# Layer 0 up-projection: normalized operand from its sixteenth unit on, evictions by ScalarE, eight modulation pieces moved to VectorE

## The reference, cut to what matters

```python
for i in range(DEPTH):                                   # DEPTH = 2
    mod = c_act @ w_mod[i] + b_mod[i]                    # six vectors of 1024
    sh1, sc1, g1, sh2, sc2, g2 = jnp.split(mod, 6, axis=-1)
    h = modulate(rmsnorm(x, norm_mix[i]), sh1, sc1)      # h * (1 + scale) + shift
    y = pool_mixer(...) if i % N_MIXERS == 0 else moba_attention(...)
    x = x + g1[:, None, :] * y
    h = modulate(rmsnorm(x, norm_mlp[i]), sh2, sc2)
    x = x + g2[:, None, :] * squared_relu_mlp(h, w_up[i], w_down[i])   # relu(h @ w_up)^2 @ w_down
```

## Time and profile before

| what | value |
|---|---|
| median of 3 runs | 1028.49 us (1027.91 to 1028.98) |
| the profiled execution, its own time | 1028.39 us |
| its span, first to last instruction | 1026.6 us, so 1.8 us lie around it |
| TensorE busy | 989.7 us, 96% of the span |
| VectorE busy | 780.7 us, 76% |
| ScalarE busy | 527.2 us, 51% |
| DMA moved | 222.28 MB, mean 217 GB/s |
| granted TensorE clock, mean | 0.989 of full |

### The profile page before, as it was taken

One profiled execution on the slowest core, in us unless ns is written; L12 is line 12 of the kernel. 1 busy time (PEld: TensorE's weight loads), 2 busy tenths in 40 slices (PEclk: granted clock), 3 DMA queues, 4 the chain that ended last, 5 costly groups with the idle time before them and its releaser, 6 DMA issues.

```text
span 1026.6 us, 19924 instructions
## 1 busy us (share of the span) xinstructions
PE 989.7 (96%) x7918; PEld 939.0 (91%) x7918; DVE 780.7 (76%) x1430; ACT 527.2 (51%) x834; POOL 1.9 (0%) x14
## 2 busy tenths in 40 slices
PE   4789999999999999999999999999999999999996
PEld 1469999999998899999999989898889999999996
DVE  4659666888767778778765889899987787777554
ACT  4247655444666566764544535468116565444343
POOL 0000000000000000000000000000000000000000
PEclk9799999999999999999999999999999999999998
DMA  9998977877464865544555436363445555555531
GB/s 376 421 421 298 365 301 275 329 305 277 136 210 126 302 245 170 197 169 164 206 203 193 137 124 244 103 228 124 164 152 200 183 173 202 200 175 193 205 124 42
DMA packets 35880, 222.28 MB, mean 217 GB/s; under 512 B 3883, under 2 KB 9180, under 8 KB 9436
## 3 DMA queue, kind: packets, MB, share of 16 engines
q1 hardware_dynamic: 35804, 221.22, 59.9%
HBM read 220.13 MB, written 1.07 MB: 215 GB/s over the span
## 4 chain that ended last, share of the span: by engine, by line
PE 93%; DMA 3%; DVE 2%; ACT 1%; issue 1%; SPq 0%; DVEq 0%; ACTq 0%
PE bank L591 24%; PE bank L597 24%; PE bank L592 24%; PE bank L923 11%; PE bank L972 3%; PE s_banks L620 2%; DMA mod_raw<-w_mod 1%; PE s_banks L972 1%; DMA raw<-weights 1%; PE s_banks L597 1%; PE s_banks L591 1%; PE s_banks L592 1%; DMA x<-x_in 0%; DVE s L1519 0%; PE bank L853 0%
## 5 line engine op out<-in xcount | busy, mean ns | idle before, releaser
L1403 DVE TENSOR_TENSOR w_lo<-raw,w_hi 128x1024 fp32r<-128x1024 f32 x268 | 324.6, 1217 | 32.0 <-ACT w_hi L1043 31.2
L1043 ACT ACTIVATE w_hi<-raw 128x1024 fp32r<-128x1024 f32 x268 | 280.1, 1051 | 110.6 <-PE bank L597 104.1
L591 PE MATMUL bank<-xg_hi,w_hi 128*128 128x258 f32 (+1 forms) x1248 | 310.4, 286 | 2.3 <-DVE w_lo L1403 2.3
L592 PE MATMUL bank<-xg_lo,w_hi 128*128 128x258 f32 (+1 forms) x1248 | 306.1, 282 | 0.0
L591 PEld LDWEIGHTS bank<-xg_hi,w_hi 128*128 128x128 f32 x1248 | 235.9, 189 | 6.8 <-issue 6.6
L592 PEld LDWEIGHTS bank<-xg_lo,w_hi 128*128 128x128 f32 x1248 | 236.4, 189 | 0.2
L597 PE MATMUL bank<-xg_hi,w_lo 128*128 128x258 f32 (+1 forms) x1248 | 180.8, 283 | 0.0
L597 PEld LDWEIGHTS bank<-xg_hi,w_lo 128*128 128x128 f32 x1248 | 162.8, 189 | 0.0
L591 PE MATMUL bank<-hid_hi,w_hi 128*128 128x256 f32 x512 | 123.5, 279 | 0.0
L592 PE MATMUL bank<-hid_lo,w_hi 128*128 128x256 f32 x512 | 123.4, 279 | 0.0
L1807 DVE SCALAR_TENSOR_TENSOR y<-u,vec,y 128x256 f32<-128x256 f32 x240 | 98.4, 477 | 0.2
(11 more groups left out here) (238 smaller groups left out, 1256.6 us busy)
## 6 DMA issues: line engine op xcount, KB each, us to landing
raw<-weights SPq DMA_DIRECT2D x157, 1024.0 KB, 5.0
mod_raw<-w_mod SPq DMA_DIRECT2D x32, 1024.0 KB, 11.4
mod_raw<-w_dots SPq DMA_DIRECT2D x16, 1024.0 KB, 8.1
toep<-bias_by_distance SPq DMA_DIRECT2D x8, 256.0 KB, 5.4
x<-x_in SPq DMA_DIRECT2D x1, 1024.0 KB, 4.9
toep<-bias_by_distance SPq DMA_DIRECT2D x8, 128.0 KB, 3.9
y_out<-yout SPq DMA_DIRECT2D x4, 256.0 KB, 2.5
c_all<-c_row SPq DMA_DIRECT2D x1, 512.0 KB, 7.6
```

Source lines behind the costliest of these rows:

```text
L591: pe.matmul(dst, hi, r_hi, start=start, stop=False, skip_group_check=True)
L592: pe.matmul(dst, hi, r_lo, start=False, stop=False, skip_group_check=True)
L1043: act.activation(pool_w_hi[:, at, :] if name == "pool" and at < 2 else w_hi[:, at % HL, :], raw[:, slot, (at % 2) * UT * P:(at % 2 + 1) * ...
L1403: ve.tensor_tensor(lo, raw[:, slot, (at % 2) * UT * P:(at % 2 + 1) * UT * P], hi.bitcast(F32), ALU.subtract).then_inc(lo_done, 1)
```

## The change

- Constants: `NORMED = 15`. From the sixteenth unit of `up0` (number 15) on, the operand is `xn_hi`, `xn_lo`, which hold the normalized, scaled and shifted x (256 columns). VectorE multiplies (`xn_product(k)`, end of step 6+k), ScalarE adds the shift and rounds (`xn_high(k)`, start of step 7+k), VectorE subtracts (`xn_low(k)`, start of step 7+k), for k = 0 to 7.
- For these 17 units VectorE's `evict` is gone; ScalarE's relu reads the PSUM bank, and a bank is free when the relu is done.
- In both `up` phases ScalarE makes `hid_hi` by a second square of `ub`, in place of VectorE's copy.
- Eight of the twelve row pieces of `up0` become dots in `up0`, after units 15, 17, 19, 20, 22, 24, 26, 29. The four that stay rows are done one at a time after units 16, 21, 25, 28. `c_all` is loaded after pair 5 and activated after unit 5.
- `xn_hi`, `xn_lo` lie where slots 3 and 4 of `mod_raw` were, so from piece 20 to piece 34 there are three slots; the order of the issues (PIECES_AFTER) is new.

```diff
+NORMED = 15
-MOD_AT = {("up0", 12): HEAD, ("up0", 20): HEAD + 1, ("up0", 28): HEAD + 2}
+ROW_AT = {("up0", 16): 0, ("up0", 21): 1, ("up0", 25): 2, ("up0", 28): 3}
+COPY_AT = {("up0", 28): HEAD}
+COLS_AT = {("up0", 30): HEAD}
+DOTS_AT = {("up0", v): d for d, v in enumerate((15, 17, 19, 20, 22, 24, 26, 29))}
+for kind in "drdddrddrdrd":                 # pieces 20 to 31: d = dots, r = row
+SLOT = [q % SLOTS for q in range(MOD_FIRST)] + [n % 3 for n in range(15)] + [(n + 3) % SLOTS for n in range(15, 28)]
-PIECES_AFTER = [5, 6, 7, 8, 10, 11, 12, 13, 14, 15, 16, 17, 18, 19, 20, 22, 23, ...
+PIECES_AFTER = [6, 7, 8, 14, 14, 15, 16, 16, 17, 17, 18, 19, 19, 20, 21, 22, 23, ...
...
@@ TensorE, bank_free, whole
+                elif name == "up0" and 8 * i + j >= NORMED + 4:
+                    pe.wait_ge(relu_done, 8 * i + j - 3)
                 for k in range(DC):
+                    if ready is not None:        # unit 15: xn_lo_done
+                        pe.wait_ge(ready, k + 1)
@@ ScalarE
+            def xn_high(k):
+                act.wait_ge(xn_mul, k + 1)
+                act.activation(xn_hi[:, k, :], newt[:, k % 2, :], ACT.Identity, bias=modv[...8 * SH2 + k...]).then_inc(xn_hi_done, 1)
             def up(name, i, j):
+                if name == "up0" and 7 <= 8 * i + j < 7 + DC:
+                    xn_high(8 * i + j - 7)
+                if name == "up0" and 8 * i + j >= NORMED:
+                    act.wait_ge(pe_units, U0[name] + 8 * i + j + 1)
+                    act.activation(ub[:, j % 2, :], out_bank(name, 8 * i + j)[:, 0:SEQ], ACT.Relu).then_inc(relu_done, 1)
+                else: (as before)
                 act.wait_ge(relu_done, 8 * i + (base + j + 1))
+                act.activation(chunk(hid_hi, 8 * i + j), ub[:, j % 2, :], ACT.Square).then_inc(hid_hi_done, 1)
+                if name == "up0" and 8 * i + j >= NORMED:
+                    act.wait_ge(hid_lo_done, 8 * i + j - 1)
                 act.activation(sb2[:, j % 2, :], ub[:, j % 2, :], ACT.Square).then_inc(sq2_done, 1)
@@ VectorE
             def hidden(name, i, j):
+                ve.wait_ge(hid_hi_done, 8 * i + (base + j + 1))
                 ve.wait_ge(sq2_done, 8 * i + (base + j + 1))
-                ve.tensor_copy(chunk(hid_hi, t), sb2[:, j % 2, :]).then_inc(hid_hi_done, 1)
+            def xn_product(k):
+                ve.scalar_tensor_tensor(newt[:, k % 2, :], x[:, k, :], gain[:, 1, k:k + 1], rstd[:, 0:SEQ], ALU.mult, ALU.mult).then_inc(xn_mul, 1)
+            def xn_low(k):
+                ve.wait_ge(xn_hi_done, k + 1)
+                ve.scalar_tensor_tensor(xn_lo[:, k, :], newt[:, k % 2, :], modv[...8 * SH2 + k...], xn_hi[:, k, :].bitcast(F32), ALU.add, ALU.subtract).then_inc(xn_lo_done, 1)
             def up(name, i, j):
-                evict(name, i, j)
                 t = 8 * i + j
+                if name == "up0" and 7 <= t < 7 + DC:
+                    xn_low(t - 7)
+                if name == "up1" or t < NORMED:
+                    evict(name, i, j)
                 (split as before)
                 hidden(name, i, j)
+                if name == "up0" and 6 <= t < 6 + DC:
+                    xn_product(t - 6)
```

More of the change, by code:

```diff
@@ L63, in _phases @@
         else:
-            by_vector += GLU_SPLIT if name == "glu" else t
+            by_vector += {"glu": GLU_SPLIT, "up0": NORMED}.get(name, t)
     return units
@@ L187, in rows_of @@
     return [(kinds, p) for p in range(ROWS)] if g is None else [(8 * kind, g) for kind in kinds]
[L190 to L195, removed]
+DOTS = [(48 + 8 * kind, p) for kind in (SC2, SH2) for p in range(4)]\
+    + [(base, p) for p in range(4) for base in (8 * G2, 48 + 8 * SC1, 48 + 8 * SH1)]\
+    + [(48 + 8 * G2, p) for p in range(4)]
+DOTS_AT = {("up0", v): d for d, v in enumerate((15, 17, 19, 20, 22, 24, 26, 29))}
+DOTS_AT.update({("down0", 8 * p + at): 8 + 3 * p + n for p in range(4) for n, at in enumerate((1, 2, 5))})
+DOTS_AT.update({("down1", 8 * p): 20 + p for p in range(4)})
+PIECES = [("rows", q) for q in range(MOD_FIRST)]
+for kind in "drdddrddrdrd":
+    PIECES.append(("dots", sum(k == "dots" for k, _ in PIECES)) if kind == "d" else ("rows", sum(k == "rows" for k, _ in PIECES)))
+PIECES += [("dots", d) for d in range(8, 24)]
+NORMED_SLOTS = (3, 4)
+SLOT = [q % SLOTS for q in range(MOD_FIRST)] + [n % 3 for n in range(15)] + [(n + 3) % SLOTS for n in range(15, 28)]
+BEFORE = [max([p for p in range(q) if SLOT[p] == SLOT[q]], default=None) for q in range(len(PIECES))]
+IN_SLOT = [sum(SLOT[p] == SLOT[q] for p in range(q + 1)) for q in range(len(PIECES))]
 ROWS_PIECE = [n for n, (kind, _) in enumerate(PIECES) if kind == "rows"]
 DOTS_PIECE = [n for n, (kind, _) in enumerate(PIECES) if kind == "dots"]
-PIECES_AFTER = [5, 6, 7, 8, 10, 11, 12, 13, 14, 15, 16, 17, 18, 19, 20, 22, 23, 24, 26, 27, 28, 30, 31, 32, 48, 49, 50, 51]
+PIECES_AFTER = [6, 7, 8, 14, 14, 15, 16, 16, 17, 17, 18, 19, 19, 20, 21, 22, 23, 24, 26, 27, 28, 30, 31, 32, 48, 49, 50, 51]
 def pieces_after(p):
@@ L252, in build @@
         cz = sb("cz", [P, DC, 64], F32, first)
-        mod_raw = sb("mod_raw", [P, SLOTS, DC * SEQ], F32, first)
+        mod_raw = sb("mod_raw", [P, 3, DC * SEQ], F32, first)
+        with ExitStack() as part:
+            mod_raw2 = sb("mod_raw2", [P, 2, DC * SEQ], F32, part)
+        half_line("xn", first)
+        xn_hi = sb("xn_hi", [P, DC, SEQ], F32R, first)
+        xn_lo = sb("xn_lo", [P, DC, SEQ], F32R, first)
+        piece_slot = [mod_raw[:, s, :] for s in range(3)] + [mod_raw2[:, s, :] for s in range(2)]
         c_all = sb("c_all", [P, D], F32, first)
@@ L360, in build @@
         relu_done = sem("relu_done")
+        xn_mul, xn_hi_done, xn_lo_done = sem("xn_mul"), sem("xn_hi_done"), sem("xn_lo_done")
         sq2_done = sem("sq2_done")
@@ L468, in piece @@
             def piece(q):
-                (kind, n), s = PIECES[q], q % SLOTS
-                if q >= SLOTS:
-                    before, m = PIECES[q - SLOTS]
+                (kind, n), s = PIECES[q], SLOT[q]
+                if BEFORE[q] is not None:
+                    before, m = PIECES[BEFORE[q]]
+                    if s in NORMED_SLOTS and BEFORE[q] < MOD_FIRST <= q:
+                        sp.wait_ge(pe_units, U0["down0"])
                     if before == "rows":
@@ L477, in piece @@
                 src = w_mod if kind == "rows" else w_dots
-                sp.dma_start(mod_raw[:, s, :], src[one(n)].rearrange("a p n -> p (a n)")).then_inc(mod_in[s], 16)
+                sp.dma_start(piece_slot[s], src[one(n)].rearrange("a p n -> p (a n)")).then_inc(mod_in[s], 16)
             def pair(p, s, base=0):
@@ L620, in row @@
                     mm = pe.matmul(row_bank[32 * c:32 * c + 32, 0:SEQ], cz[:, k, 31 - r:63 - r],
-                                   mod_raw[:, n % SLOTS, SEQ * k:SEQ * (k + 1)], start=r == 0 and k < 4,
+                                   piece_slot[SLOT[n]][:, SEQ * k:SEQ * (k + 1)], start=r == 0 and k < 4,
                                    stop=r == ROW_COUNT[b] - 1 and k >= 4, tile_position=(0, 32 * c), skip_group_check=True)
@@ L640, in mod_work @@
             def mod_work(name, v):
-                if (name, v) in MOD_AT:
-                    rows(MOD_AT[name, v])
+                if (name, v) in ROW_AT:
+                    row(HEAD, ROW_AT[name, v])
                 if (name, v) in COLS_AT:
@@ L773, in down @@
                 dst = out_bank(name, j // 4)
-                if j % 4 == 0:
+                if name == "down0" and i == 0 and j % 4 == 0:
+                    pe.wait_ge(relu_done, 29 if j == 0 else 32)
+                elif j % 4 == 0:
                     pe.wait_ge(tile_read, 2 * i + (T0[name] + j // 4 - (1 if not isinstance(i, int) or i or j else 3)))
@@ L804, in step @@
                 def step(i, j):
-                    whole(name, i, j, xg_hi, xg_lo, SEQ + 2)
+                    v = 8 * i + j
+                    if name == "up0" and v >= NORMED:
+                        whole(name, i, j, xn_hi, xn_lo, SEQ, xn_lo_done if v == NORMED else None)
+                    else:
+                        whole(name, i, j, xg_hi, xg_lo, SEQ + 2)
                     if isinstance(i, int):
-                        mod_work(name, 8 * i + j)
+                        mod_work(name, v)
                 unrolled = 32 if name == "up0" else 16
@@ L1053, in mod_work @@
             def mod_work(name, v):
-                if (name, v) in MOD_AT:
-                    mod_copy(MOD_AT[name, v])
-                if (name, v) == ("up0", 16):
+                if (name, v) in COPY_AT:
+                    mod_copy(COPY_AT[name, v])
+                if (name, v) == ("up0", 5):
                     act.wait_ge(c_row_in, 16)
```

22 lines of the change are left out of this document (12 added, 10 removed).

## The result

| | before | after |
|---|---|---|
| median (range, runs) on one chip | 1028.47 us (1027.91 to 1028.98, 5) | 1034.38 us (1032.69 to 1034.94, 5) |
| profiled execution, its own time | 1028.39 us | 1032.69 us |
| its span and mean granted clock | 1026.6 us, 0.989 | 1030.9 us, 0.983 |

The ratio is 1.0058 [1.0047, 1.0070]: slower, as forecast. The medians differ by 5.9 us, the profiled executions by 4.3; that of after is the fastest of its five. The forecast was 1037.3 in 1030 to 1042.

A forecast was written before the change was run, and what follows sets the result against it. TensorE was taken as the bound, 93% of the chain. Savings -9.4, loop stall +11.2, clock +1.7, late piece +3.6, clock +1.7 gave +8.8 us on 1028.39: forecast 1037.3 us, range 1030.0 to 1042.0.

The forecast's parts named there:

- The loop: up0 steps 7 to 14, VectorE and ScalarE waiting in turn: 3.58 us a turn, TensorE stalls 11.2 us up to unit 15.
- The late piece: up0 row 21 waits for piece 25, behind pair 15: stall 5.3 us, 3.6 after the first clock loss.
- Savings: TensorE in up0: fewer rows and columns, -8.3 us, and 17 units at 2.83 in place of 2.89, -1.1: together -9.4 us.
- Clock: TensorE's clock drops after each of the two long up0 stalls: 1.7 us charged to each (0 to 2.5).
- At nothing: Items priced at zero: second square in up1, second wait before hid_lo, bank waits, end of up0, slots 3 and 4, head.
- the stretch from 1032 to 1035: Total between rival 1 and the forecast: second stall without clock loss, or a turn of 3.4 us; chance 0.14.
- 1, no second stall: up0: only the first stall, pieces land in time and the clock stays up; +1.8 us, 1030.3; chance 0.13.
- 2, the loop doesn't bind: up0: turns of 3.1 us and landing within 6 us, so faster: 1025.8, or 1019.0 with no stall; chance 0.08.
- the places named: Sign in up0: TensorE idle at unit 11 (about 2 us) and at unit 15's seventh and eighth chunk for xn_lo.
- 3, VectorE as the bound: After unit 15 of up0: late landings, dots waiting for pieces, clock loss three times; +12 to +15 us, 1040 to 1043; chance 0.13.
- 4, 256 columns save nothing: TensorE in up0 not relieved as said: 1 us more, inside the range; no chance given.

The follow-up runs named there:

- Undoing the order: Changed kernel with the product one step earlier, xn_high behind ScalarE's squares, xn_low behind the evict: 1026.83 us, ratio 0.9988 to the kernel before.
- the second trace of after: The changed kernel run again, unedited: 1032.97 us, ratio 1.0051 to the kernel before.
- small dots: Changed kernel with the eight dots of up0 acting on 8 columns in place of 1024: 1033.04 us, ratio 1.0049 to the kernel before.

## Why the prediction was right

**The loop.** Forecast 3.58 us a turn, measured 3.62. `xn_low(7)` was to start at 122.4 and started at 121.16; its execution was 1.56 us ahead at unit 4. Stall forecast 11.2 with 1.7 of clock: 12.9. Measured by units of TensorE: unit 10 to 11 +2.65 over 2.89, 11 to 14 +2.2, 14 to 15 +7.2, 15 to 16 +1.1 of slower clock: 13.1. Undoing the order took 7.6 of it away (5.5 stay by the same units), and the late piece took 1.8 of that back. One link was not the one I named: by the chain, ScalarE's split stood until 116.92 ahead of `xn_high`, where I had it free. In the turn at 101.92 the product reached `xn_high` at 102.43 (0.51 later, as in rows 7), so both arrived together. In the last turn, which has no split, the chain goes through `hid_lo` and the product, and it is no shorter (117.46 to 121.16).

**The late piece.** Forecast 3.6 and 1.7 of clock, 5.3; measured 4.6 in units: 2.89 of waiting and 1.46 more at row 21, at a granted clock of 0.66, and 0.26 at row 25, of which 0.18 is a wait for piece 28. Pair 15 was to leave 2.6 us after unit 18's end, the piece 0.4 later: it left 2.6 later (136.73 against 134.15) and 0.37. But two sizes were off and nearly cancelled: the piece was ready 8.4 us after its issue (137.10 to 145.52), not 10.7; and the 1.7 that I took off, because the first clock loss would give SP more time, was not there, since the clock was back before unit 17 (granted 1.00 from 126.2 to 130 us). This term is also the least steady: by the same units it is 3.6 in the second trace of after and 6.2 with `hid` put back.

**Savings.** Forecast -9.4, measured -8.6. A single row costs TensorE 1.19 us between two units (4.02 for 2.83), so four cost 4.8, where I had 4.0 (3.79 for the batch and 0.2). The two batches, two `cols` and 17 shorter units are as read from rows 3.

**Clock.** 1.7 was charged to each stall. Beyond the waits, the units show 2.4 around unit 15 (1.3 and 1.1) and 1.5 after row 21, with granted clocks of 0.53 and 0.66 in the rows above. The 1.3 isn't all clock: at units 12 to 14 a wait of 0.31 makes a unit 0.73 longer at a granted clock of 1.00. And not every stall cost clock: after the 1.91 us at unit 11 it stayed at 1.00 (98.8 to 117.4 us), and after a wait of 2.44 at row 21 in the second trace of after too (146.2 to 150 us). So a flat 1.7 a stall is a charge that came out about right, not a rule that these runs show. The Trainium skill (Perfetto Trace Analysis, Matmul Optimizations) says that the matmul engine scales its power with utilization. The clocks of 0.53 and 0.66 fit that, the 1.00 after unit 11 does not show it. The Trainium skill's drain of 1.38 us beside a table load (ScalarE: Activation LUTs, What ACT_TABLE_LOAD costs) is absent again: 2.26 us held load and activation.

**Sum.** 13.1 + 4.6 - 8.6 = +9.1 in `up0` (9.2 by the stretch), forecast +8.8 (12.9 + 5.3 - 9.4). The late piece was put 0.7 too high and the savings 0.8 too high, and these two cancel. With `hid` put back at its old place within 256 bytes the whole kernel was 10.6 us above the kernel before on the same chip (1037.82 against 1027.24), its `up0` 10.8 longer than in the trace of before: 1.8 us more than forecast, by the late piece.

**What the forecast did not have.** "At nothing" stood a list with slots and head. It did not ask where the buffers behind the split `mod_raw` would land. `hid` moved by 128 bytes and `down1` gained 3.4 us. So the sum was right for `up0` and wrong for the whole: the term that was missing is -3.4 under "at nothing". The time of 1034.4 lies in the range, but in the stretch from 1032 to 1035, which the forecast gave 0.14 for other reasons (a second stall without clock loss, or a turn of 3.4 us); neither came, and the addresses put it there. Without them the ratio of 1.0105 on 1028.47 gives 1039.3 (an estimate), 2 above the forecast and still in the range. That the change is slower, and why, doesn't rest on this luck.

**The rivals.** 1, no second stall: the DMA wait of 2.89 is against it. 2, the loop doesn't bind: three waits at just the places named. 3, VectorE as the bound: no wait for `w_lo` after unit 14, and small dots gained nothing. 4, 256 columns save nothing: units are 2.83. The DMA engines without free time from 137 to 160 us are in none of the four; the forecast put the late piece down to its issue and a landing of 10.7 alone.

**Open.** With `hid` at the new place `down1` was at 2.72 in ten of ten traces, `down0` in three only, with the same operand; with the old place both were at 2.83 in all four. `w2` went between 2.72 and 2.83 with its operand where it was. So a second factor exists, which no run here tells. All but the changed kernel have one trace each, so it isn't known either whether `down0` and `w2` change pace from kernel to kernel or from execution to execution. Why the place matters is open too.

## What to carry to other kernels

When a step is put on two engines in turn, add up one turn by the starts in their timelines and hold it against the stage's unit: the same instructions cost 3.62 or 2.60 us a turn by their order, and an average busy share of 76 and 53% shows nothing of it. A transfer that is tied to a step of a lagging engine is late by that lag; look at the share of the DMA engines too, for where it is 1.00, as here, relieving that engine only moved the wait to the next transfer in the queue. After any edit of buffers compare the pace of stages that were not edited, and separate a gift of addresses from the change by a pad.

## What was not expected of the hardware

- In `down1` the place of the moving operand within 256 bytes of a partition went with the pace of a matmul of 256 columns, 117.8 or 113.2 ns (2.83 and 2.72 us for 24), in all 14 traces, without a wait or a lower clock. 128 bytes alone made the kernel 0.7% faster.
- At the same addresses a stage can run at either pace (`down0`, `w2`).
- A stall of 1.91 us at unit 11 left the granted clock at 1.00, one of 2.89 us at row 21 was followed by 0.66.
- 16 row matmuls cost 1.19 us when they stand alone between two units, and 0.95 each in a batch of four (3.79).
